# Order of splits, waits and reductions in the attention and the two mixers of a two-block transformer kernel

## The chip, the cores and the metric

The kernel runs on one core of one Trainium2 chip. The metric is the device time of one execution, in microseconds. The core has five engines that run their own instruction lists and meet only at semaphores: PE (TensorE, matrix products), ACT (ScalarE), DVE (VectorE), POOL (GpSimd) and SP (SyncE, which here only starts DMA transfers).

## What is computed

The reference applies two transformer blocks to 256 tokens of width 1024, in float32, batch one. `first_block` has two layers on two streams (256 latent and 256 context tokens): layer 0 is feed-forward, gated MLP, feed-forward; layer 1 is feed-forward, attention, feed-forward. `second_block` has two layers on one stream, each of them feed-forward, mixer, feed-forward. Cut to what the change touches:

```python
def gqa_mix(...):                      # attention of the first block, 8 query heads, 2 key heads, 512 keys
    qkv = h_lat @ w_qkv; kv_c = h_ctx @ w_qkv[:, Q_DIM:]
    q = apply_rope(rms_norm(heads(q)), cos, sin)
    y = softmax(q @ k.T * hd ** -0.5) @ v @ w_o

def mixer(h):                          # one sublayer of the second block
    u = h @ mix_w_in                   # q, k, v, conv a and g, gla q, k, v, gate, rank-16 decay gate
    att  = causal_softmax(rope(rms(q)) @ rope(rms(k)).T) @ v           # 8 heads of 64
    conv = silu(layernorm(causal_conv31(a * sigmoid(g))))              # 256 channels, 31 taps
    gla  = chunked_gated_linear_attention(q, k, v, decays)             # 4 heads, chunks of 64
    return concat(att, conv, gla) @ mix_w_out
```

Each sublayer has a scale, a shift and a gate that come from `silu(c) @ ada_w` (`w_mod` in the first block), nine vectors of 1024 in a layer.

## The kernel before

**Weights.** Every weight matrix is cut into units of 128 by 2048 float32 (1 MB). A unit goes through four steps. SP loads it with two 512 KB transfers into `wraw` (L514). ACT copies it, rounded, into `wh` (the high part, `split_next`, L834). DVE subtracts to get `wl`, the low part (`split_next`, L1219). PE multiplies with three products, high times high, high times low and low times high. There are two slots for each of the three buffers. The load of a unit waits until the low part two units earlier is made (`wlo_done`), the high part waits for the load and for PE to be through with the unit two earlier (`w_used`), and PE waits for the low part (`wlo_done`). `split_next(u)` on ACT or DVE makes the parts of unit u+1; so `unit(i)` of these engines splits one unit ahead of the one that PE's `unit(i)` multiplies.

**Modulation.** The vectors of the next sublayer are summed on DVE in 12 steps for each sublayer: `mod_unit` (L1192) takes 1 MB of `mraw` that SP loaded (L499) and makes two scalar-tensor-tensor instructions. In a mixer the step of index `MIX_MODS` is done in DVE's `unit(idx)`, and SP starts its transfer after the load of two units later. SP's list is in order: each load waits for its slot, and what stands behind it waits as well. `mod_end`, `factors` and `columns` (PE, L2065) turn the sums into columns.

**Order of work.** Nothing is scheduled at run time: each engine's list of a sublayer is written out by hand, in the branch for its kind, between the two feed-forward sublayers.

**Attention** (sublayer 4). Weight units 0 and 1 make keys and values, units 2 to 5 the queries (two heads each), and units 6 to 9 are the output matrix. PE's list (L2546 on) goes `k_t`, `turn_queries(0)`, `unit(4)`, `scores(0)`, `turn_queries(1)`, `unit(5)`, `turn_queries(2)`, `scores(1)`, then the heads. For each pair of query heads DVE's `queries` normalises and rotates (L1748 a sum of squares, then a wait for POOL's `power`, L670, then L1754 to L1764). `maximum` (L1779) takes the row maximum of a head's scores, ACT exponentiates, `normalise` (L1784, L1787) divides. DVE's `unit(4)`, `unit(5)` and `unit(6)` stand between these; `unit(5)` is the split of unit 6 (by the numbers of a unit in the sublayer), `unit(6)` that of unit 7. POOL has only five `power` calls there (L787 to L792).

**Mixer** (sublayers 7 and 10). Twelve input units, then four output units (`out(0)` to `out(3)`, units 12 to 15, L2617 to L2628). PE sums the squares of x (L2646), broadcasts the factors by `rows_of_factors` (L2113, behind POOL's `power`), then `unit(0)`, the small product for the decay gate `cg` (L2655, needs DVE's `cgl`), `unit(1)`, `unit(2)`, and so on, with the products of the three branches between the units. `unit(i)` of PE is L2579 for its first product and L2185 for the others. The convolution's first 128 channels are 31 matrix products with diagonal matrices that ACT makes (L1087). Its second 128 channels are taken by POOL: from `ch_t` on it does, for each of 31 taps, a tensor-scalar (L804) and an addition (L810), with the two `power` calls (L670) for the norms of queries and keys after the taps that `MIX_POOL_TAPS` (L58) gives. When the last addition is done PE transposes the result (L2749). The end of the mixer: DVE normalises the three softmaxes `c`, `b`, `a` (L1895 maximum, L1903, L1904), PE transposes the weights (L2617) and multiplies by v (L2776, L2778), ACT and DVE make the high and low parts of the three results (`hi_...`, L1105; `lo_...`, L1909), and `out(0)` wants `lo_gla`, `out(1)` `lo_conv`, `out(2)` and `out(3)` `lo_att`.

`keep_going(bank, n)` (L2094) makes n products of 128 by 128 whose result nothing reads. `Stages` (L361 for DVE) numbers the marks of an engine: a mark's place in the list is the order in which it is raised.

Of the kernel before, what the change touches and what calls it, by code (L numbers as in the profile page):

```python
# [57 lines left out]
MIX_POOL_TAPS = (11, 16, 31)  # L58
# [121 lines left out]
def program(nc, ins, out, subs):  # L180
    u_end = subs[-1]["n_unit"] + dict(ffn=33, gmlp=36, attn=10, mix=16)[subs[-1]["kind"]]
    with ExitStack() as ctx:
# [89 lines left out]
        def gm_halves(m):  # L272
# [89 lines left out]
                                    "norm_c stats lo_gla pt_c norm_b o_conv max_a pt_b norm_a pt_a lo_conv lo_att")  # L362
# [293 lines left out]
        def _(pool):  # L656
# [72 lines left out]
            for s in subs:  # L729
# [58 lines left out]
                elif s["kind"] == "attn":  # L788
                    load_ln(s)
                    power(nrm1[:, 16:24], 8)  # L790
                    for u in range(4):
                        power(nrm1[:, 4 * u:4 * u + 4], 4)  # L792
                elif s["kind"] == "mix":
# [31 lines left out]
        def _(act):  # L825
# [69 lines left out]
            for s in subs:  # L895
# [77 lines left out]
                elif s["kind"] == "attn":  # L973
# [48 lines left out]
                    unit(3, False)  # L1022
                    square(1)
                    copy_heads(0)
                    unit(4)
# [22 lines left out]
                elif s["kind"] == "mix":  # L1048
# [5 lines left out]
                    def unit(i, to=None):  # L1054

                        split_next(u0 + i)
                        if i == 0:
                            act.wait_ge(mix_full, 160 * (turn + 1) + 32)
                            MA.done("cgh", act.activation(cgh, cg_raw, ACT.Copy))
                        if i < 12:  # L1060
# [9 lines left out]
                            else:  # L1070
                                act.activation(proj[:, :, at:at + CW], src, ACT.Copy).then_inc(pair_free, 1)
                        if i < 10:
# [46 lines left out]
                    unit(3)  # L1119
# [12 lines left out]
                    unit(7)  # L1132
                    MP.wait(act, "heads", turn)
                    stage("q2", act.activation(q2.rearrange("p a b -> p (a b)"), ps[:, 2:4].rearrange("p a b -> p (a b)"), ACT.Copy))
                    unit(8)
# [10 lines left out]
                    high("gla", 6, (6,))  # L1146
                    unit(12)
                    exps("a", 0, p_a[:], 12)
# [17 lines left out]
        def _(dve):  # L1166
# [354 lines left out]
            for s in subs:  # L1521
# [214 lines left out]
                elif s["kind"] == "attn":  # L1736
# [78 lines left out]
                    unit(5)  # L1815
# [3 lines left out]
                    unit(6)  # L1819
                    for h in range(HEADS):  # L1820
# [7 lines left out]
                        if h + 2 < HEADS:  # L1828
                            normalise(h + 2)
                    unit(7)  # L1830
# [7 lines left out]
                elif s["kind"] == "mix":  # L1838
# [5 lines left out]
                    def unit(i):  # L1844
                        if i < 15:
                            split_next(u0 + i)
                        if i == 5:
# [72 lines left out]
                    unit(0)  # L1920
# [3 lines left out]
                    stage("cgl", dve.tensor_tensor(cgl, cg_raw, cgh.bitcast(F32), ALU.subtract))  # L1924
                    if turn == 0:
# [9 lines left out]
                    unit(2)  # L1935
# [5 lines left out]
                    unit(3)  # L1941
                    MA.wait(dve, "softplus", turn)
                    stage("g", dve.tensor_tensor(gg[:], e2[:], e1[:], ALU.subtract))
                    unit(4)
                    sum_squares(0)
                    turn_heads(0)
                    unit(5)
# [3 lines left out]
                    unit(7)  # L1951
# [868 lines left out]
```

## Time and profile before

| what | value |
|---|---|
| median of 3 runs | 3186.78 us (3181.14 to 3188.61) |
| the profiled execution, its own time | 3186.64 us |
| its span, first to last instruction | 3184.9 us |
| PE busy | 3079.7 us, 97% of the span |
| DVE busy | 2031.3 us, 64% |
| ACT busy | 958.2 us, 30% |
| POOL busy | 693.3 us, 22% |
| mean granted TensorE clock | 0.985 |
| attention | about 1664.6 to 1794.2 us of the span |
| first mixer | about 2215 to 2398 us |
| second mixer | about 2800 to 2981 us |

The span is the profiled execution from its first to its last instruction; its own time has 1.7 us more, which lie around the span. [...] The two mixers run from the sum of squares to the last output product, and the attention from its first unit to its last.

### The profile page before, as it was taken

To read this page: it belongs to the slowest core of one execution; us is meant where nothing else is said; L and a number is where in the kernel's file an instruction comes from. 1 tells how busy PE (TensorE), PEld (TensorE's weight loads), DVE (VectorE), ACT (ScalarE), POOL (GpSimd) and SP (SyncE) were. 2 spreads that over 40 slices of the span, in tenths; PEclk is the share of its full clock that TensorE was granted. 3 is DMA by queue.
4 is the path that set the end of the run, shared out by engine and by line. 5 is a ranking of instruction groups with operands and counts; after the bars stand their busy time and mean duration, and the time that the engine had idled before them with its cause. 6 is when DMAs were issued, how large, how long until landed. Compare 5 with 4: busy or idle time off the path is not lost.

```text
span 3184.9 us, 46705 instructions
## 1 busy us (share of the span) xinstructions
PE 3079.7 (97%) x19332; PEld 2738.2 (86%) x19332; DVE 2031.3 (64%) x2134; ACT 958.2 (30%) x1006; POOL 693.3 (22%) x640
## 2 busy tenths in 40 slices
PE   8999999999999999999998999999889999998999
PEld 5888889888888888888887798899879999987899
DVE  5854368766387434774556765775777758668664
ACT  2211122212221122221214333333434343353333
POOL 1311100224022010220100121330742313147110
PEclk9999999999999999999999999999989999999999
DMA  7633235232255332553523496685547869654464
GB/s 258 216 128 93 95 117 197 95 106 80 90 160 173 101 99 87 161 176 119 172 96 131 142 280 205 202 265 172 185 149 233 267 201 272 221 172 172 137 182 158
DMA packets 501667, 522.78 MB, mean 164 GB/s; under 512 B 15732, under 2 KB 433830, under 8 KB 501478
## 3 DMA queue, kind: packets, MB, share of 16 engines
q1 hardware_dynamic: 498536, 513.76, 50.4%
q0 software_dynamic: 2944, 6.32, 0.9%
q8 instruction: 143, 2.34, 0.3%
q14 instruction: 44, 0.36, 0.0%
HBM read 518.97 MB, written 1.05 MB: 163 GB/s over the span
## 4 chain that ended last, share of the span: by engine, by line
PE 85%; DVE 8%; POOL 3%; ACT 2%; issue 1%; DMA 1%; SPq 0%; DVEq 0%; ACTq 0%; POOLq 0%
PE ps L2157 29%; PE ps L2331 15%; PE ps L2243 15%; PE ps L2355 8%; PE ps L2185 6%; PE ps L2222 2%; DVE wl L1219 2%; POOL wst L804 1%; PE ps L2201 1%; POOL lnp L810 1%; PE ps L2269 1%; PE ps L2065 1%; PE ps L2628 1%; ACT wh L834 1%; PE ps L2094 1%
## 5 line engine op out<-in xcount | busy, mean ns | idle before, releaser
L1219 DVE TENSOR_TENSOR wl<-wraw,wh 128x2048 fp32r<-128x2048 f32 x341 | 835.0, 2449 | 586.3 <-ACT wh L834 580.9
L834 ACT ACTIVATE wh<-wraw 128x2048 fp32r<-128x2048 f32 x341 | 652.5, 1914 | 930.5 <-PE ps L2243 387.5
L2157 PE MATMUL ps<-xh,wh 128*128 128x512 f32 (+1 forms) x1504 | 564.5, 375 | 0.7 <-DVE wl L1219 0.4
L2157 PE MATMUL ps<-xl,wh 128*128 128x512 f32 (+1 forms) x1504 | 552.7, 367 | 0.0
L2157 PE MATMUL ps<-xh,wl 128*128 128x512 f32 (+1 forms) x1504 | 551.3, 367 | 0.0
L2331 PE MATMUL ps<-xh,wh 128*128 128x258 f32 x1408 | 403.4, 287 | 5.8 <-DVE xl L1417 4.6
L673 POOL CAST hh<-ht 128x256 f32 (+1 forms) x176 | 140.1, 796 | 1221.3 <-DVE ht L1599 887.0
L2331 PE MATMUL ps<-xh,wl 128*128 128x258 f32 x1408 | 399.5, 284 | 0.0
L2331 PE MATMUL ps<-xl,wh 128*128 128x258 f32 x1408 | 399.3, 284 | 0.0
L1192 DVE SCALAR_TENSOR_TENSOR acc<-mraw,svec,acc 128x1024 f32<-128x1024 f32 x259 | 343.0, 1344 | 15.4 <-DMA mraw<-in_ada_w 10.2
L2157 PEld LDWEIGHTS ps<-xl,wh 128*128 128x128 f32 x1504 | 282.9, 188 | 49.3
L2157 PEld LDWEIGHTS ps<-xh,wl 128*128 128x128 f32 x1504 | 283.3, 188 | 45.1 <-issue 0.7
L2157 PEld LDWEIGHTS ps<-xh,wh 128*128 128x128 f32 x1504 | 283.3, 188 | 44.8 <-issue 1.8
L2331 PEld LDWEIGHTS ps<-xh,wh 128*128 128x128 f32 x1408 | 268.6, 191 | 10.9 <-DVE xl L1417 7.6
L2331 PEld LDWEIGHTS ps<-xl,wh 128*128 128x128 f32 x1408 | 268.9, 191 | 0.0
L2331 PEld LDWEIGHTS ps<-xh,wl 128*128 128x128 f32 x1408 | 268.5, 191 | 0.0
L2185 PE MATMUL ps<-wh,xh 128*128 128x256 f32 x832 | 244.0, 293 | 22.8 <-DVE wl L1219 22.7
L932 ACT ACTIVATE sg<-ps 128x512 f32<-128x512 f32 (+1 forms) x88 | 47.9, 545 | 660.2 <-PE ps L2157 629.2
L2185 PE MATMUL ps<-wh,xl 128*128 128x256 f32 x832 | 238.0, 286 | 0.0
L2185 PE MATMUL ps<-wl,xh 128*128 128x256 f32 x832 | 237.9, 286 | 0.0
L674 POOL TENSOR_TENSOR hl<-ht,hh 128x256 f32 (+1 forms) x176 | 219.2, 1246 | 29.2 <-POOL hh L673 29.2
L2243 PE MATMUL ps<-wh,hh 128*128 128x512 f32 x520 | 205.2, 395 | 1.3 <-DVE wl L1219 1.3
(426 smaller groups left out, 5530.0 us busy)
## 6 DMA issues: line engine op xcount, KB each, us to landing
wraw<-in_ffn_w_in SPq DMA_DIRECT2D x352, 512.0 KB, 5.2
wraw<-in_ffn_w_out SPq DMA_DIRECT2D x176, 512.0 KB, 4.2
mraw<-in_ada_w SPq DMA_DIRECT2D x72, 1024.0 KB, 6.9
mraw<-in_w_mod SPq DMA_DIRECT2D x64, 1024.0 KB, 6.3
wraw<-in_gmlp_w_in SPq DMA_DIRECT2D x48, 512.0 KB, 4.4
wraw<-in_mix_w_in SPq DMA_DIRECT2D x48, 512.0 KB, 4.7
wraw<-in_gmlp_w_out SPq DMA_DIRECT2D x24, 512.0 KB, 3.8
first_w<-in_w_mod SPq DMA_DIRECT2D x8, 1024.0 KB, 11.6
```

The source lines that it names most:

```text
L673: steps.link(pool.tensor_copy(hh[:, where], ht[:, par, 0:width]))
L674: pool.tensor_tensor(hl[:, where], ht[:, par, 0:width], hh[:, where].bitcast(F32), ALU.subtract)\
L834: act.activation(wh[:, slot], wraw[:, slot], ACT.Copy).then_inc(whi_done, 1)
L932: act.activation(sg[:, pair, 0:W], ps[:, 2 * pair, 0:W], ACT.Silu).then_inc(sg_ready, 1)
L1192: op = dve.scalar_tensor_tensor(out=to, in0=mraw[:, q % 2, jj], scalar=svec[:, v, 2 * q + jj:2 * q + jj + 1], in1=biasrow[:] if q == jj == ...
L1219: dve.tensor_tensor(wl[:, slot], wraw[:, slot], wh[:, slot].bitcast(F32), ALU.subtract)\
L2157: m = pe.matmul(ps[:, bank, 0:width], a, b, start=k == p == 0, stop=k == KD - 1 and p == 2)
L2185: m = pe.matmul(to, a, b, start=k == p == 0, stop=k == KD - 1 and p == 2)
L2222: m = pe.matmul(ps[:, 2 * t + half], a, b, start=False, stop=i == kk == 1 and p == 2, skip_group_check=i == 0)
L2243: m = pe.matmul(ps[:, bank0 + 2 * t + half], a, b, start=start and kk == p == 0, stop=stop and kk == 1 and p == 2, skip_group_check=not st ...
L2331: m = pe.matmul(ps[:, 2 * pair + r, 0:XW], a, b, start=n == p == 0, stop=n == KD - 1 and p == 2)
L2355: m = pe.matmul(ps[:, j, 0:T], a, b, start=i == kk == p == 0, stop=i == KF // 2 - 1 and kk == 1 and p == 2, skip_group_check=i == 5)
```

## The change

It touches the attention's and the mixers' branches on all five engines' lists except SP's, which is left as it is written. There are six edits.

1. Attention: PE does `unit(4)` and `unit(5)` earlier, ACT makes the high part of unit 5 before it squares the keys, and the low parts of units 6 and 7 are made by POOL, after its last `power`, no longer by DVE, which waits for both before its `unit(7)`.
2. Mixer, start: `keep_going(3, 8)` before and `keep_going(3, 14)` after `rows_of_factors`; `cgh` (ACT) and `cgl` (DVE) are made ahead of the first split.
3. Mixer, splits: units 3 and 4, 6, and 8 and 9 are split ahead of modulation, turning of heads and other work on DVE, and 4 and 9 ahead on ACT. `qk` is marked one step earlier (on `kt`).
4. POOL's two `power` calls come after 9 and 14 taps in place of 11 and 16. The second half's 31 taps stay on POOL, as they were.
5. Mixer, end: DVE takes `maximum("a")` behind `normalise("c")`, ACT makes the exponentials of `a` ahead of its `unit(12)`, DVE normalises `a` right behind `o_conv`.
6. Mixer, end: DVE's split of unit 13 (its `unit(12)`) moves behind the two `turned_weights`, its modulation behind `low("conv")`.

```diff
-MIX_POOL_TAPS = (11, 16, 31)
+MIX_POOL_TAPS = (9, 14, 31)
...
@@ POOL, attention
                         power(nrm1[:, 4 * u:4 * u + 4], 4)
+                    for i in (6, 7):
+                        u = s["n_unit"] + i
+                        pool.wait_ge(whi_done, u + 1)
+                        pool.tensor_tensor(wl[:, u % 2], wraw[:, u % 2], wh[:, u % 2].bitcast(F32), ALU.subtract)\
+                            .then_inc(wlo_done, 1)
@@ ACT, attention
                     unit(3, False)
+                    split_next(u0 + 4)
                     square(1)
                     copy_heads(0)
-                    unit(4)
+                    unit(4, False)
@@ ACT, mixer
-                        split_next(u0 + i)
                         if i == 0:
                             act.wait_ge(mix_full, 160 * (turn + 1) + 32)
                             MA.done("cgh", act.activation(cgh, cg_raw, ACT.Copy))
+                        if split:
+                            split_next(u0 + i)
...
+                        if i == 2:
+                            split_next(u0 + 3)
...
-                    unit(3)
+                    unit(3, False)
...
                     unit(7)
+                    split_next(u0 + 8)
                     MP.wait(act, "heads", turn)
...
-                    unit(8)
+                    unit(8, False)
...
+                    exps("a", 0, p_a[:], 12)
                     unit(12)
-                    exps("a", 0, p_a[:], 12)
@@ DVE, attention
                     normalise(0)
-                    unit(5)
                     maximum(1)
                     queries(3)
                     normalise(1)
-                    unit(6)
...
+                    dve.wait_ge(wlo_done, u0 + 9)
                     unit(7)
@@ DVE, mixer
-                    unit(0)
...
                     stage("cgl", dve.tensor_tensor(cgl, cg_raw, cgh.bitcast(F32), ALU.subtract))
+                    unit(0)
...
-                    unit(2)
+                    split_next(u0 + 2)
+                    split_next(u0 + 3)
                     MP.wait(dve, "z", turn)
...
-                    unit(3)
+                    modulation(2)
                     MA.wait(dve, "softplus", turn)
                     stage("g", dve.tensor_tensor(gg[:], e2[:], e1[:], ALU.subtract))
+                    modulation(3)
                     unit(4)
                     sum_squares(0)
+                    split_next(u0 + 5)
                     turn_heads(0)
-                    unit(5)
+                    modulation(5)
                     sum_squares(1)
                     unit(6)
                     turn_heads(1)
-                    unit(7)
+                    split_next(u0 + 7)
+                    split_next(u0 + 8)
+                    modulation(7)
...
-                    dve.tensor_tensor(kt[:], c_k, e2[:], ALU.mult)
+                    stage("qk", dve.tensor_tensor(kt[:], c_k, e2[:], ALU.mult))
+                    modulation(8)
...
-                    unit(8)
                     MP.wait(dve, "qk_t", turn)
...
                     normalise("c", p_c, 0)
+                    maximum("a", 0, 4, 12)
                     MP.wait(dve, "conv", turn)
...
                     normalise("b", p_b, 8)
-                    unit(12)
...
                     stage("o_conv", last)
-                    maximum("a", 0, 4, 12)
+                    normalise("a", p_a[:], 12)
                     turned_weights("b", 2, slice(2, 4))
-                    normalise("a", p_a[:], 12)
                     turned_weights("a", 0, slice(0, 2))
+                    split_next(u0 + 12)
                     low("conv", 4, (2,))
+                    modulation(12)
                     unit(13)
@@ PE, attention
+                    unit(4)
                     turn_queries(0)
-                    unit(4)
+                    unit(5)
                     scores(0)
                     turn_queries(1)
-                    unit(5)
                     turn_queries(2)
                     scores(1)
@@ PE, mixer
                     m.then_inc(ss_ready, 1)
+                    keep_going(3, 8)
                     rows_of_factors(s)
+                    keep_going(3, 14)
                     unit(0)
```

## Rows read from the trace of the kernel before

**Rows 1.** The page's chain that ended last: share of the span by engine.

```profile
PE 85%; DVE 8%; POOL 3%; ACT 2%; issue 1%; DMA 1%; SPq 0%; DVEq 0%; ACTq 0%; POOLq 0%
```

**Rows 2.** The chain of waits in attention: start us, us, what.

```profile
1713.21 2.29 DVE wl L1219
1727.98 2.20 DVE wl L1219
1732.25 1.02 POOL nrm L670
1737.48 2.20 DVE wl L1219
1739.68 1.15 DVE negm L1779
```

**Rows 3.** POOL's instructions of the kind that splits: ns min/median/max, and their shapes.

```profile
L674 POOL TENSOR_TENSOR hl<-ht,hh x176: 725/1285/3362, 66.6 to 3122.4; 128x256 f32 x110, 128x512 f32 x66
...
L787 POOL TENSOR_TENSOR gm_h<-ht,gm_h x8: 1293/2268/3423, 748.3 to 789.5; 128x512 fp32r<-128x512 f32 x8
```

**Rows 4.** POOL's and DVE's timeline at 282 us: start us, us.

```profile
282.22 1.29 POOL L674 TENSOR_TENSOR hl<-ht,hh 128x512 f32 x1 [0.16 <-POOL hh L673]
...
282.29 3.37 DVE L1219 TENSOR_TENSOR wl<-wraw,wh 128x2048 fp32r<-128x2048 f32 x1 [1.02 <-ACT wh L834]
```

**Rows 5.** The timeline of DVE and POOL at 789 us.

```profile
789.45 2.29 DVE L1219 TENSOR_TENSOR wl<-wraw,wh 128x2048 fp32r<-128x2048 f32 x1
...
789.47 3.42 POOL L787 TENSOR_TENSOR gm_h<-ht,gm_h 128x512 fp32r<-128x512 f32 x1
```

**Rows 6.** What PE waited for in the first mixer: us in total, times, longest.

```profile
PE ps L2185 <- DVE wl L1219: 11.2, 3, 4.3
PE ps L2617 <- DVE p_a L1904: 5.9, 1, 5.9
...
PE ps L2655 <- DVE cgl L1924: 1.1, 1, 1.1
```

**Rows 7.** What PE waited for in the second mixer.

```profile
PE ps L2185 <- DVE wl L1219: 9.8, 3, 4.1
...
PE ps L2655 <- DVE cgl L1924: 1.6, 1, 1.6
```

**Rows 8.** What DVE waited for in the first mixer.

```profile
DVE proj L1881 <- POOL nrm L670: 6.4, 2, 4.9
```

**Rows 9.** PE's timeline and its granted clock (seventh figure of a window).

```profile
1670.18 3.73 PE L2094 MATMUL ps<-ident,ones 128*128 128x128 f32 x32
...
2218.00:2223.00 5.00, 2.36 (x10) 1.98 (x9) 1.52 (x5) 0.91 (x2) 1.65 (x2) 0.50 0.09 6
```

**Rows 10.** POOL's timeline in the first mixer: first tap, last tap.

```profile
2249.59 1.22 POOL L804 TENSOR_SCALAR lnp<-lnp 128x256 f32<-128x256 f32 x1 [19.41 <-ACT lnp L1082]
...
2344.17 0.73 POOL L810 TENSOR_TENSOR lnp<-lnp,wst 128x256 f32<-128x256 f32 x1
```

**Rows 11.** POOL's last tap in the second mixer.

```profile
2926.62 0.72 POOL L810 TENSOR_TENSOR lnp<-lnp,wst 128x256 f32<-128x256 f32 x1
```

**Rows 12.** PE's transposes of the convolution, first and second mixer.

```profile
2350.37 0.60 PE L2749 MATMUL ps<-ident,lnp 128*128 128x128 f32 x4
...
2931.21 0.60 PE L2749 MATMUL ps<-ident,lnp 128*128 128x128 f32 x4
```

**Rows 13.** DVE's timeline at the end of the first mixer.

```profile
2366.49 2.29 DVE L1219 TENSOR_TENSOR wl<-wraw,wh 128x2048 fp32r<-128x2048 f32 x1
...
2386.03 2.60 DVE L1192 SCALAR_TENSOR_TENSOR acc<-mraw,svec,acc 128x1024 f32<-128x1024 f32 x2
2388.55 1.22 DVE L1909 TENSOR_TENSOR xl<-ps,xh 128x1024 fp32r<-128x1024 f32 x1
```

**Rows 14.** SP's transfers there, and the page's time to landing (last figure).

```profile
2369.65 0.43 SPq L499 DMA_DIRECT2D mraw<-in_ada_w  x1
...
mraw<-in_ada_w SPq DMA_DIRECT2D x72, 1024.0 KB, 6.9
```

More of the change, by code:

```diff
@@ L361, in program @@
         MV = Stages(sem("mix_dve"), "cgl cg_t h absz g sum_q q_turned sum_k k_turned qk k2 kt_t states max_c o_copy max_b oc "
-                                    "norm_c stats lo_gla pt_c norm_b o_conv max_a pt_b norm_a pt_a lo_conv lo_att")
+                                    "norm_c max_a stats lo_gla pt_c norm_b o_conv norm_a pt_b pt_a lo_conv lo_att")
         MP = Stages(sem("mix_pe"), "cg z h_t sums heads qk_t scores o s_c s_b conv s_a omt pt_c pt_b pt_a convt pv")
@@ L1053, in stage, with unit @@
                         MA.wait(act, name, turn)
-                    def unit(i, to=None):
-                        split_next(u0 + i)
+                    def unit(i, split=True):
                         if i == 0:
@@ L1846, in unit, with modulation @@
                             split_next(u0 + i)
+                        modulation(i)
+                    def modulation(i):
                         if i == 5:
@@ L1960, in _ @@
                                                       in1=e3[:], op0=ALU.mult, op1=ALU.mult)
-                    stage("qk", op)
+                    steps.link(op)
                     MP.wait(dve, "heads", turn)
                     stage("k2", dve.tensor_copy(k2.rearrange("p a b -> p (a b)"), ps[:, 4:6].rearrange("p a b -> p (a b)")))
-                    unit(8)
                     MP.wait(dve, "qk_t", turn)
```

## Prediction, made before the changed kernel was run

> **What bounds the kernel now.** I read the page's chain first: 85% of the span is PE's own work, 8% DVE's, 3% POOL's [rows 1]. So the kernel is bound by PE, save for the two kinds of stage that the change touches. Then I read the chain of waits inside the attention, where two low parts (2.20 us each) and a row maximum of DVE stand on it [rows 2]: there DVE sets the pace. Then what PE waited for in each mixer. It lost 11.2 us in three waits for a low part in the first mixer, 9.8 us in the second, and 1.1 and 1.6 us for `cgl` [rows 3, 4]. That is what edits 2 and 3 aim at. Last I asked what is late next: POOL's taps run without a gap from 2249.59 to 2344.90 in the first mixer [rows 5], and PE's transposes of their result start at 2350.37 there and at 2931.21 in the second [rows 6], where the taps end at 2927.34 [rows 7]. PE can be earlier there by 5.5 and 3.9 us and no more, however many waits are removed ahead of it.
>
> **Attention (edit 1).** PE's `unit(5)` moves ahead of `scores(0)` and `unit(4)` ahead of `turn_queries(0)`. DVE's low part of unit 5 starts now at 1713.21, because ACT makes its high part only after other work; with the high part made early it follows the turning of the queries at about 1709.5. The first maximum comes behind PE's scores, which stand behind one unit more, so I keep only 1.1 of these 3.7 us. DVE then drops two low parts. The first, at 1727.98, gives 0.6 us, not 2.2, since `maximum(1)` needs `scores(1)`, which PE does only behind `turn_queries(2)`; the second, at 1737.48, gives its 2.2 us. So the third maximum, which ends at 1740.83 [rows 2], would end 3.8 us earlier (1.07 + 0.58 + 2.20), at 1737.0, if POOL's part cost nothing.
>
> It costs something. POOL has a 128x256 subtraction in 0.725 us at least, a 128x512 one in 1.285 [rows 8], so 256 columns more are 0.56 us, and 2048 columns (eight times 256) are 0.725 + 7 x 0.56 = 4.65 us, an estimate; four times the 128x512 one is 5.1, the upper bound. POOL starts on them when its last `power` is done, about 1731.5 (now 1732.25 + 1.02, 1.65 earlier), just where DVE turns the last queries, with two-input instructions on SBUF. The trace shows what such a pair does: at 282.22 POOL began a subtraction of 1.29 us, DVE's low part began 0.07 us later and took 3.37 us in place of 2.29, so 1.08 longer [rows 9]. The other way about, a POOL subtraction that began behind a DVE low part took 3.42 us where 1.28 to 1.29 is the least [rows 8, 10]. So the one that comes second stands until the first is through. The longest such block of DVE in any row is one POOL instruction, about 1.3 us; if nothing longer than this happens, the two subtractions cost DVE 2.6 us and the edit still gives 3.8 - 2.6 = 1.2 us. If the block lasts as long as POOL's instruction, DVE loses 4.65 twice, 9.3 us less the little that lies beside DVE's own waits: the queries' last turning ends at about 1744, `normalise(1)` at 1745, the third maximum at 1746.2 in place of 1740.83, 5.4 us later. Between these ends I take the longer one, because the rows show the block to follow the length of POOL's instruction and to let DVE in only at its end. The head loop behind it is paced by the same DVE chain, so the delay stays: **+5.4 us**, bounds -3.8 and +6.4 (5.1 us for each subtraction).
>
> The Trainium skill, "SBUF — State Buffer", section "Who interferes with whom", has the same as a rule: the port pair that DVE and GpSimd share is an exclusive lock, held for the whole instruction, and a DVE instruction with two SBUF inputs contends with a GpSimd one that reads SBUF. By that rule the block is the full length, as in the sum above; the trace agrees at 1.3 us (3.37 against 2.29), and no row of it shows 4.65. The rule speaks against this edit; by the other reading of the rows (1.3 us each) the edit would come to -1.2.
>
> **Mixers, start (edit 2).** 22 products are added in each mixer. 32 of their instructions took 3.73 us at full clock [rows 11], 0.117 each, and a product is two of them, so 22 cost 5.1 us at the most, if they stand in PE's way. They don't quite: PE waits there for POOL's `power` and DVE's first columns. The clock granted in the first mixer is at its lower level, 1.2 GHz (0.50), from 2218 to 2223 already [rows 11], before the place where the products go. I put the later end of `unit(0)` at +1.4 us if the clock stays down and -0.3 if they bring it back. `cgl` ahead of the split removes 1.1 and 1.6 us of waiting [rows 3, 4]. Together nothing, between +3 and -2 in each mixer.
>
> **Mixers, splits (edits 3 and 4).** The split of the next unit stood behind modulation (2.6 us) or turned heads; with it ahead, the 11.2 and 9.8 us of waiting mostly go, some 9 us. POOL's taps don't shorten: 31 taps in 95.3 us are 3.1 us each [rows 5], and they start with `ch_t`, on ACT, which now has one split (1.9 us) ahead of it. The first `power` two taps earlier takes what DVE waits for in turning heads (6.4 us [rows 12]) away or leaves it to the split that stands there now; it moves nothing on POOL. So the end of taps comes 1.6 us later in the first mixer and 0.5 in the second, and PE's transposes can be earlier by 5.5 - 1.6 = 3.9 and 3.9 - 0.5 = 3.4 us. Of this the cold start of a unit behind a wait may take 1.5 in the first.
>
> **Mixers, end (edits 5 and 6).** The maximum and exponentials of `a` moved ahead remove PE's wait of 5.9 us for `p_a` [rows 3], and PE reaches `out(1)` some 5 us earlier. But the low part of unit 13, which starts at 2366.49 now, comes behind both `turned_weights`: by my count of DVE's instructions at 2376.5, ten us later, and ends at 2378.8. It gates SP: the load of unit 15 and then `mraw` of the last modulation go out right behind it, `mraw` now at 2369.65, 0.9 us after the low part's end, to land 6.9 us later by the page's median [rows 13, 14]. So it goes out at 2379.7 and lands at 2386.6; the modulation takes 2.60 us, to 2389.2, and the low part of the attention's result, queued behind it on DVE, 1.22 us, to 2390.4. Now it ends at 2388.55 + 1.22 = 2389.8 [rows 13], and `out(2)` starts at 2390.5 when PE is through with `out(1)`. So `out(2)` starts when it did: what PE gains in `out(0)` and `out(1)` it gives back in one wait of some 5 us, and behind such a wait it may run at half clock at first, which I put at 1.5 us: a unit takes 5.9 us at full clock and 7.4 where part of it is at half. In the second mixer `out(2)` starts 1.1 us later than this now, and I keep that as gain.
>
> **The sum.** What is gained ahead of the transposes (3.9 and 3.4 us) is kept at the end, since everything behind them shifts with them. In the first mixer I take off 1.5 us for the cold unit ahead of them and 1.5 for a cold `out(2)`: 3.9 - 3.0 = 0.9 us. In the second I take off 1.5 for `out(2)` and add the 1.1 of its tail: 3.4 - 1.5 + 1.1 = 3.0 us. Together -3.9 us, bounds -9.4 (5.5 + 3.9, all the room there is) and +3 (edit 2's upper price in one mixer, nothing gained in the other). With +5.4 from attention: +1.5. The profiled execution took 3186.64 us with a span of 3184.9; it stands 0.14 under the median of 3186.78, so both give **3188** (3186.6 + 1.5). A measurement of this kernel can tell about 0.2% from no change, 6.4 us, so this is no change.
>
> **Rivals.** (A) Faster: POOL's subtractions cost DVE little (they fall into DVE's waits, or it gets in between), and the mixers give all of POOL's room. For it: the longest block in the rows is 1.3 us, and DVE waits in that stretch for `power`. Against it: the rows' blocks are as long as POOL's instruction. It gives 3186.6 - 1.2 - 9.4 = 3176, or 3173.4 with -3.8 in place of -1.2. With the mixers at -3.9 it is 3182, still no change. 0.25. (B) Slower: POOL's taps become the mixer's end. DVE's work is packed denser, each low part that meets a tap holds it up (one more meeting is 1.8 us by the tap's mean of 3.1), the taps end later and PE waits for `cacc`. It decides from the point where the taps take more than about 99 us (95.3 + the 3.9 that are left). Then a mixer gives +1.5 to +2 and the whole is 3186.6 + 5.4 + 3.5 = 3195.5. For it: the room is 5% of the taps' time. Against it: what is moved is the same work at other times. 0.18. (C) The change doesn't do what it says at the start: the products are put where the clock is already down, cost 1.5 us each mixer, and bring nothing. That alone gives 3191; it stays inside no change and is part of the forecast's range.
>
> **Chances.** Forecast (give and take) 0.57, A 0.25, B 0.18. From the same cases: faster by over 0.2% (below 3180.4) 0.25, within 0.57, slower (above 3193.2) 0.18. Range: up to 3196 for B, down to 3176 for A's first price; the deepest part of A is left out. The forecast's own range is 3181 to 3193.
>
> **What would show it.** In the attention: two POOL subtractions of 4.6 to 4.7 us with DVE instructions of 4 to 5 us beside them where 0.4 stands now, and the third maximum 5 us later. If DVE's stay below 1.5 us, that step is wrong and the stage is shorter. In the mixers: PE's waits for `wl` down from 11.2 and 9.8 to under 3; the transposes 2 to 4 us earlier against the mixer's start, with POOL's last tap within 1 us of them; a new PE wait of some 5 us before `out(2)` for `lo_att`, with DVE behind `mraw`. If the transposes come 6 us earlier, POOL's taps got shorter and the forecast is too high. A wait of PE or ACT for `cacc` is B.

## The result, and the profile after

In the prediction some groups of rows are named by numbers other than those they stand under. There, [rows 3] is group 6, 4 is 7, 5 is 10, 6 is 12, 7 is 11, 8 is 3, 9 is 4, 10 is 5, 11 is 9 and 12 is 8; 1, 2, 13 and 14 are the same. From here on every number is that of the group as it stands.

The changed kernel took **3196.13 us** (median of 7 runs, 3188.18 to 3202.43), the kernel before 3183.57 (7 runs, 3180.05 to 3189.15). The ratio is **1.0035**, 95% interval 1.0024 to 1.0047, so 11 us slower (7.6 to 15). The forecast was 3188 and no change. 3196.13 lies at the upper end of the full range, which stood at 3196 for the slower rival, and outside the forecast's own range of 3181 to 3193. The change is clear of the 0.2% that the text asked for: it came out as the slower case, which had 0.18. The profiled execution took 3194.63 us with a span of 3192.9, 8.0 us more than that of before; the parts below add up to these 8.0. Single executions of one kernel differ by some microseconds, as the ranges show.

The page of the changed kernel, busy time and the chain that ended last:

```profile
PE 3090.6 (97%) x19420; PEld 2749.6 (86%) x19420; DVE 2037.4 (64%) x2132; ACT 958.3 (30%) x1006; POOL 707.2 (22%) x642
...
PE 84%; DVE 7%; POOL 4%; ACT 2%; DMA 1%; issue 1%; SPq 0%; DVEq 0%; ACTq 0%; POOLq 0%
```

POOL's share of the chain rose from 3% [rows 1] to 4%. To see where the time went I took the starts of ACT's high parts, which come in the same order and number in both kernels, and subtracted. In the profiled executions, between the same two high parts around attention: 192.13 us before, 198.79 after (**+6.7**). From the first sum of squares of a mixer to a high part in the feed-forward behind it: 192.61 and 192.60 in the first (**0.0**), 194.01 and 195.70 in the second (**+1.7**); in the second mixer the stretch ends one high part later than in the first, so only kernels are to be compared in it, not the two mixers. The rest (-0.4) lies in stages whose code is the same.

**Attention.** The chain of waits of the kernel before, at the turning of the last queries:

```profile
1733.29 0.70 DVE ql L1754
...
1734.01 0.42 DVE tm L1759
```

and of the changed kernel, from the second maximum on:

```profile
1728.17 1.22 DVE negm L1789
...
1730.33 1.02 POOL nrm L670
1731.37 5.00 DVE ql L1764
1736.39 4.60 DVE tm L1769
1740.99 0.34 DVE tm L1770
```

and POOL's timeline in the same stretch:

```profile
1731.30 9.41 POOL L796 TENSOR_TENSOR wl<-wraw,wh 128x2048 fp32r<-128x2048 f32 x2
```

Two DVE instructions that took 0.70 and 0.42 us in the kernel before take 5.00 and 4.60, side by side with POOL's two subtractions, which are 4.7 us each. The attention was 1.7 us early when it began (1632.07 against 1633.77 at the high part ahead of it), so the third maximum, which ends at 1745.17 and ended at 1740.83 [rows 2], is 6.0 us late against its own start.

**Mixers.** What PE waited for, first mixer:

```profile
PE ps L2646 <- DVE xl L1921: 10.5, 2, 6.2
PE ps L2203 <- DVE wl L1229: 5.1, 3, 4.0
```

and second mixer:

```profile
PE ps L2646 <- DVE xl L1921: 9.2, 2, 4.9
PE ps L2203 <- DVE wl L1229: 5.0, 3, 4.0
PE ps L2769 <- POOL lnp L815: 1.9, 1, 1.9
```

The waits for a low part of a weight fell from 11.2 and 9.8 us [rows 6, 7] to 5.1 and 5.0, and those for `p_a` and `cgl` are gone. The prediction's sign was a fall to under 3 us. One wait of 4.0 us stays in each mixer: DVE makes the low part of unit 7 behind `turn_heads(0)`, which still waits for POOL's `power` (4.65 us in the first mixer; both waits for `power` there come to 8.3 us, and were 6.4 before [rows 8]), and PE waits for that low part. In their place stand waits for `xl` in the output units (10.5 and 9.2 us, one of 2.9 before) and one for POOL's taps. POOL's last tap and PE's transposes of it, first mixer, and then the second:

```profile
2349.02 0.72 POOL L815 TENSOR_TENSOR lnp<-lnp,wst 128x256 f32<-128x256 f32 x1
...
2351.73 0.60 PE L2769 MATMUL ps<-ident,lnp 128*128 128x128 f32 x4
...
2936.94 0.72 POOL L815 TENSOR_TENSOR lnp<-lnp,wst 128x256 f32<-128x256 f32 x1
...
2937.81 0.63 PE L2769 MATMUL ps<-ident,lnp 128*128 128x128 f32 x4 [1.95 <-POOL lnp L815]
```

Against the mixer's first sum of squares (at 2214.79 and 2221.10; 2800.14 and 2806.44) the transposes moved from 135.58 to 130.63 us in the first mixer (4.95 earlier) and from 131.07 to 131.37 in the second (0.3 later). Then the end of the first mixer, on DVE, SP and PE:

```profile
2378.75 2.28 DVE L1229 TENSOR_TENSOR wl<-wraw,wh 128x2048 fp32r<-128x2048 f32 x1
...
2381.90 0.43 SPq L499 DMA_DIRECT2D mraw<-in_ada_w  x1
...
2390.01 2.60 DVE L1202 SCALAR_TENSOR_TENSOR acc<-mraw,svec,acc 128x1024 f32<-128x1024 f32 x2 [3.29 <-DMA mraw<-in_ada_w]
2392.53 1.22 DVE L1921 TENSOR_TENSOR xl<-ps,xh 128x1024 fp32r<-128x1024 f32 x1
...
2393.90 0.55 PE L2646 MATMUL ps<-xh,wh 128*128 128x256 f32 x1 [6.22 <-DVE xl L1921]
```

Read from the top: the late low part of unit 13, the transfer behind it, DVE's wait for the transfer, the low part of the attention's result behind that, and PE's wait for it. From silu's end (ACT's silu of the gate, behind the last input unit; at 2358.66, and 2357.30 before) to the same high part in the feed-forward behind the mixer it is 55.04 us where it was 50.10: the 4.95 us gained at the transposes are given back to the last tenth. In the second mixer it is 52.63 against 51.24.

### The profile page after: what moved, and what is told of

Read it like the earlier page. It is cut to its first block, busy times and chain, and to the rows that moved or that the text cites. A ratio compares the mean times of both kernels' runs of the same rounds, so it can differ in the third digit from the quotient of the medians.

```text
span 3192.9 us, 46882 instructions
## 1 busy us (share of the span) xinstructions
PE 3090.6 (97%) x19420; PEld 2749.6 (86%) x19420; DVE 2037.4 (64%) x2132; ACT 958.3 (30%) x1006; POOL 707.2 (22%) x642
## 3 DMA queue, kind: packets, MB, share of 16 engines
HBM read 518.97 MB, written 1.05 MB: 163 GB/s over the span
## 4 chain that ended last, share of the span: by engine, by line
PE 84%; DVE 7%; POOL 4%; ACT 2%; DMA 1%; issue 1%; SPq 0%; DVEq 0%; ACTq 0%; POOLq 0%
PE ps L2175 29%; PE ps L2349 15%; PE ps L2261 15%; PE ps L2373 8%; PE ps L2203 6%; PE ps L2240 2%; POOL wst L809 2%; DVE wl L1229 2%; POOL lnp L815 2%; PE ps L2219 1%; PE ps L2646 1%; PE ps L2112 1%; PE ps L2287 1%; PE ps L2083 1%; ACT wh L839 1%
```

## The experiments

Twelve kernels ran. "Attention" is the stretch above; "mixers" are the two stretches from the first sum of squares; "end" is from silu's end to a high part behind (in the second mixer one earlier than that of "mixers"). All three come from one profiled execution of each. The ratios are of timed runs against the kernel before on the same chip.

| kernel | ratio (95% interval) | attention | mixers | end, 1st and 2nd |
|---|---|---|---|---|
| before | 1 | 192.1 | 192.6, 194.0 | 50.1, 51.2 |
| changed | 1.0035 (1.0024 to 1.0047) | 198.8 | 192.6, 195.7 | 55.0, 52.6 |
| e1 edit 1 alone | 1.0024 (1.0011 to 1.0036) | 197.4 | 191.6, 190.3 | 51.0, 50.1 |
| e2 low parts on DVE | 1.0022 (1.0012 to 1.0033) | 192.0 | 193.6, 197.5 | 55.0, 51.5 |
| e3 unit 13 early | 0.9988 (0.9979 to 0.9997) | 197.6 | 184.7, 189.4 | 47.1, 46.6 |
| e4 no keep_going | 1.0034 (1.0021 to 1.0048) | 197.6 | 187.9, 198.5 | 51.9, 53.8 |
| e5 = e2 + e3 | 0.9974 (0.9964 to 0.9985) | 191.9 | 185.5, 188.1 | 46.1, 47.1 |
| e6 POOL after q_3 | 1.0041 (1.0029 to 1.0053) | 198.7 | 191.6, 199.2 | 54.9, 53.2 |
| e7 = e5, old attention | 0.9978 (0.9969 to 0.9987) | 192.1 | 185.6, 189.2 | 46.1, 46.1 |
| e8 = e5, ch_t first | 0.9968 (0.9955 to 0.9980) | 190.8 | 185.8, 189.3 | 46.8, 46.1 |
| e9 edits 2 to 4 alone | 1.0007 (0.9996 to 1.0018) | 192.5 | 188.5, 195.8 | 51.1, 51.1 |
| e10 edit 5 alone | 0.9986 (0.9976 to 0.9996) | 193.7 | 187.6, 191.6 | 48.3, 48.3 |
| e11 = e5, 25 taps | 0.9952 (0.9936 to 0.9967) | 192.0 | 178.2, 188.9 | 47.2, 47.2 |
| e12 eight pieces | 1.0026 (1.0014 to 1.0037) | 195.3 | 192.4, 195.6 | 54.7, 52.7 |

How far one execution of a mixer can be trusted: before and e1 have the same mixers and differ by 1.0 and 3.7 us; the changed kernel, e2, e6 and e12 have the same ones and span 2.0 us in the first (191.6 to 193.6) and 3.6 in the second (195.6 to 199.2). Attention is steadier (191.9 to 192.5 wherever it should be as before, but for 190.8 in e8 and 193.7 in e10, where its code gives no reason). With the whole of edit 1 it spans 197.4 to 198.8 in four kernels (changed, e1, e3, e4), 197.9 in the mean, against 192.6 in the four with none of it (before, e7, e9, e10). So the cost of edit 1 in attention is 5.3 us by these means, and the +6.7 of the single pair is at its upper end. The mixers of the changed kernel, e2, e6 and e12 come to 389.5 us together in the mean, those of before and e1 to 384.3: +5.3, where the single pair shows +1.7.

### Attention: is it POOL's block, and how long is it?

**e1.** The kernel before with edit 1 and nothing else.

> The kernel before with edit 1 alone (attention: unit 5 moved forward, two low parts on POOL). Theory (a full-length block of DVE by POOL's two subtractions): the stage is 6 to 7 us longer than before, DVE instructions of 4.5 to 5 us in it, and the whole 6 to 7 us slower, ratio 1.0020. Rival (what the profile of the changed kernel shows in attention is drift of one execution, and the loss is in the mixers): the whole stays within 2 us of before, ratio 1.000 to 1.0006.

1.0024, 7.6 us, with attention at 197.4: the theory. Edit 1 by itself is some two thirds of the whole loss.

**e2.** The changed kernel, with POOL's loop removed:

```diff
-                    for i in (6, 7):
-                        u = s["n_unit"] + i
-                        pool.wait_ge(whi_done, u + 1)
-                        pool.tensor_tensor(wl[:, u % 2], ...).then_inc(wlo_done, 1)
...
                     normalise(0)
+                    unit(5)
                     maximum(1)
                     queries(3)
                     normalise(1)
+                    unit(6)
...
-                    dve.wait_ge(wlo_done, u0 + 9)
```

> The changed kernel with the low parts of units 6 and 7 back on DVE; PE's and ACT's new order stays. Theory (the block is the loss): the attention's third maximum comes 6 to 7 us earlier than in the changed kernel, and the whole is about 3189 us against its 3196. Rival (the new order, with unit 5 ahead of the first scores, is the loss): less than 2 us comes back, about 3195.

Attention fell from 198.8 to 192.0. All of its loss is POOL's part, and the new order of unit 5 is worth nothing by itself. Beside this, e2 shows what the rest of the change does alone: with attention as before it is still 1.0022, so edits 2 to 6 cost 7 us (3.8 to 10.5). The whole came to 3191.6, 2.6 us above what I expected (its second mixer ran 1.8 us longer than the changed kernel's in this execution).

**e7** asks the same from the other side: e5 (below) without any of edit 1.

> As e5, and also PE's and ACT's order in attention as before (edit 1 gone altogether). Theory (unit 5 forward gives nothing by itself, since the first maximum is earlier by 1.1 us and the second isn't): within 1 us of e5 in attention and in all, about 3177. Rival (unit 5 forward gives 1 to 3 us that POOL's block hid): 2 us or more slower than e5.

192.1 against 191.9, medians 3177.15 and 3177.73. The rival falls.

**e6.** POOL works when DVE has turned its last queries.

```diff
+                    AV.wait(pool, "q_3", 0)
                     for i in (6, 7):
```

> The changed kernel, but POOL's two subtractions wait until DVE has turned the last queries (mark q_3). Theory (DVE is blocked only where it reads two inputs from SBUF or moves SBUF to SBUF at twice the rate): the two long waits on DVE's chain move from the turning to the head loop; normalise (SBUF to SBUF) may stand for 4 us, the maxima and low parts that read PSUM don't; of the 6.6 us in attention some 3 come back, total about 3193. Rival 1 (any DVE instruction is blocked, so it doesn't matter where POOL works): attention stays within 1 us of 198.8. Rival 2 (nothing in the head loop is blocked): attention at 190 to 192, total 3189.

The theory's size was wrong: nothing came back (198.7; 1.0041). POOL's and DVE's timeline:

```profile
1738.62 9.13 POOL L797 TENSOR_TENSOR wl<-wraw,wh 128x2048 fp32r<-128x2048 f32 x2 [3.19 <-DVE ql L1775]
...
1738.78 9.26 DVE L1798 TENSOR_SCALAR ht<-ht,den 128x512 f32<-128x512 f32 x2
```

The block doesn't need two inputs. `normalise` has one input, from SBUF to SBUF, two instructions that take 0.88 us together elsewhere, and they took 9.26: one for each of POOL's. Since the very next instruction of DVE in the head loop is of that kind, moving POOL's work behind the turning only changes who stands. The rival that any instruction is blocked has the right length, but this run doesn't prove it: no maximum or low part that reads PSUM fell beside POOL's work here. In e12 they do, and they are not blocked (below).

**e12.** The same work of POOL in pieces.

```diff
-                        pool.tensor_tensor(wl[:, u % 2], wraw[:, u % 2], wh[:, u % 2].bitcast(F32), ALU.subtract)\
-                            .then_inc(wlo_done, 1)
+                        for c in range(8):
+                            cut = slice(c * 256, (c + 1) * 256)
+                            op = pool.tensor_tensor(wl[:, u % 2, cut], wraw[:, u % 2, cut], wh[:, u % 2, cut].bitcast(F32), ALU.subtract)
+                        op.then_inc(wlo_done, 1)
```

> The changed kernel, with each of POOL's two subtractions in attention cut into eight of 128x256. Theory (the port is held for one instruction and handed over at its end): DVE's blocked instructions are 0.5 to 0.8 us longer each, not 4.6; the six of the turning and the two of normalise stand once each, so DVE loses 5 to 6 us, not 9, and attention is 194 to 196 us against 198.8. Rival 1 (the block costs what POOL works in all, however it is cut): 198 to 200. Rival 2 (POOL is always the one that waits when its pieces are short): 191 to 192.

195.3: inside the theory's 194 to 196. DVE and POOL take turns, as the chain of waits shows (0.83 and 0.88 us for what takes 0.34 and 0.42), and POOL needs 13.07 us for its sixteen pieces where the two whole ones took 9.41:

```profile
1735.61 1.22 DVE ql L1766
1736.83 0.02 issue
1736.85 0.83 DVE tm L1771
1737.68 0.88 DVE tm L1772
```

```profile
1735.54 13.07 POOL L798 TENSOR_TENSOR wl<-wraw,wh 128x256 fp32r<-128x256 f32 x16
```

So the block lasts as long as the one POOL instruction, and the length of that instruction is the price. 3.5 us of the 6.7 come back, or some 2.5 against the mean of 197.9; DVE doing the work itself gives all of it (e2).

This run also settles what e6 left open. DVE's maximum and a low part, both of which read PSUM, fall beside POOL's pieces:

```profile
1743.66 1.21 DVE L1791 TENSOR_REDUCE negm<-ps 128x2 f32<-128x1024 f32 x1
...
1746.66 0.42 DVE L1836 TENSOR_TENSOR xl<-ps,xh 128x256 fp32r<-128x256 f32 x1 [1.79 <-ACT xh L1051]
```

```profile
1744.28 2.77 POOL L798 TENSOR_TENSOR wl<-wraw,wh 128x256 fp32r<-128x256 f32 x4
```

They take 1.21 and 0.42 us, the same as where POOL is idle (1.22 and 0.42), and POOL's four pieces take 0.72 each. So not any instruction of DVE is blocked: those with two inputs in SBUF are, and `normalise`, and these two are not. The four pieces also give the price of the cutting: they follow each other at 0.69 us, which makes 11.0 for sixteen, an estimate, of the 13.07.

### The end of the mixers: what holds out(2)?

**e3.** One line moved back.

```diff
                     normalise("b", p_b, 8)
+                    split_next(u0 + 12)
...
                     turned_weights("a", 0, slice(0, 2))
-                    split_next(u0 + 12)
                     low("conv", 4, (2,))
```

> The changed kernel with DVE's low part of unit 13 back behind normalise b; the rest of the mixer's end as changed. Theory (the late low part holds SP's load and mraw, and mraw the last modulation and lo_att): mraw goes out some 8 us earlier, PE's wait of 4.9 to 6.2 us before out(2) goes, out(2) runs in 5.9 us and not 8.6, and each mixer is 6 us shorter: about 3184 in all. Rival (DVE's own work at the end is the limit): the low part only moves 2.3 us of DVE's time forward, lo_att comes no earlier, and the whole stays within 2 us of 3196.

0.9988 against 1.0035: 15 us for one line, where I had expected 12. The end of the first mixer now:

```profile
2373.72 2.28 DVE L1229 TENSOR_TENSOR wl<-wraw,wh 128x2048 fp32r<-128x2048 f32 x1
...
2376.88 0.43 SPq L499 DMA_DIRECT2D mraw<-in_ada_w  x1
...
2389.30 2.60 DVE L1202 SCALAR_TENSOR_TENSOR acc<-mraw,svec,acc 128x1024 f32<-128x1024 f32 x2
...
2393.18 0.36 PE L2646 MATMUL ps<-xh,wh 128*128 128x256 f32 x1 [1.05 <-DVE xl L1921]
```

Against silu's end (2363.12 here, 2358.66 in the changed kernel) the transfer goes out at 13.8 us and not 23.2, the last modulation has no wait, and `out(2)` starts at 30.1 and not 35.2. It also runs at the clock's upper level. The granted clock of the stretch of `out(2)`, first the changed kernel and then e3, is the seventh figure:

```profile
2393.90:2402.50 8.60, 8.60 (x51) 8.60 (x51) 2.05 (x1) 0.00 (x0) 0.00 (x0) 0.65 0.44 122
```

```profile
2393.20:2399.10 5.90, 5.90 (x51) 5.90 (x51) 2.29 (x1) 0.94 (x1) 0.00 (x0) 1.00 0.43 112
```

The ends are shorter by 7.9 and 6.0 us (55.0 to 47.1 and 52.6 to 46.6); in the first mixer 5.2 of them are the earlier start of `out(2)` and 2.7 its faster run.

**e5.** e2 and e3 together.

> The changed kernel with both: low parts 6 and 7 on DVE, and the low part of unit 13 back behind normalise b. Theory (two separate losses that add): attention as in the kernel before (192 us between the same high parts), mixers as with the early split alone, about 3177 us, ratio 0.9975. Rival (the mixers' length hangs on something else, such as the moment at which they start): they fall back to 180 us each, and the whole is about 3190.

3177.7, ratio 0.9974: the two losses are separate and add, and the version beats both kernels.

**e10.** Edit 5 alone, with unit 13 where the kernel before has it.

> The kernel before with edit 5 alone (maximum and exponentials of a moved ahead), the low part of unit 13 where it was. Theory (edit 5 is the part that pays): silu's end to the end of the mixer is 44 to 45 us, as with the early split, against 47.7 before: 3 us less in each, 3178 in all. Rival (PE's wait of 5.9 us for p_a goes in full): 6 us in each, 3172.

0.9986, 4.5 us, and ends of 48.3 and 48.3 against 50.1 and 51.2. That is 1.8 and 2.9 us less, where I had 3 in each; the 44 to 45 and the 47.7 that I wrote are counted to an earlier point (the first product of the feed-forward). e5 and e7 have 46.1 to 47.1. What their ends have on top is that the modulation of unit 13 comes behind `low("conv")`, the other half of edit 6, which would be worth 1 to 2 us in each mixer; but these kernels also have edits 2 to 4, and no run takes that half alone, so this is argued and not shown.

### The front of the mixers: what do the splits give?

**e9.** Edits 2 to 4, with attention and the end as before.

> The kernel before with edits 2 to 4 alone (start and splits of the mixers, powers two taps earlier); attention and the mixer's end as before. Theory (POOL's taps bound what these edits can give): the transposes of the convolution start 128.5 to 132 us behind the first sum of squares, within 0.2 to 2 us of POOL's last tap, 5 us earlier than before in the first mixer and 0 to 1 in the second; 4 us off in all, 3180. Rival (removing 9 us of PE's waits in each mixer shows in full once the end is left alone): 12 us or more off, 3171.

A miss in size: 1.0007, 0.9996 to 1.0018, so between 1.3 us faster and 5.7 slower, where I had 4 us faster. The rival of 12 us is out. The transposes do what the theory says. First and second mixer:

```profile
2340.33 0.73 POOL L810 TENSOR_TENSOR lnp<-lnp,wst 128x256 f32<-128x256 f32 x1
...
2341.20 0.63 PE L2763 MATMUL ps<-ident,lnp 128*128 128x128 f32 x4 [0.19 <-POOL lnp L810]
...
2923.50 0.63 PE L2763 MATMUL ps<-ident,lnp 128*128 128x128 f32 x4 [1.92 <-POOL lnp L810]
```

At 130.38 us behind the sum of squares in the first mixer, against 135.58, and PE has come to wait for POOL in both.

**e11.** e5 with POOL's last six taps left out of the computation.

```diff
-MIX_POOL_TAPS = (9, 14, 31)
+MIX_POOL_TAPS = (9, 14, 25)
...
-                                if tap == CONV_K:
+                                if tap == MIX_POOL_TAPS[-1]:
```

> As e5, but POOL takes 25 of the second half's 31 taps; the last six are left out of the computation. Theory (POOL's taps are the mixer's bound at the transposes): POOL ends 11 to 18 us earlier, the transposes start at about 124 us behind the first sum of squares, where PE gets there by itself, 5 to 6 us earlier than in e5, with no wait for the taps; 10 to 12 us off in all, 3166. Rival (PE or DVE is the bound there, and POOL only near it): within 2 us of e5, 3176.

0.9952: 7 us less than e5, not 10 to 12. In the first mixer POOL ends at 2338.40, and PE's transposes start at 2347.92, 124.0 us behind the sum of squares, within 0.2 us of where PE was ready in e5 (130.66 less its wait of 6.49). In the second they start at 2924.87, 130.0 us behind, with POOL through since 2909.01: no gain at all. The difference is the clock in the stretch ahead of them, first mixer, then second:

```profile
2328.00:2348.00 20.00, 19.64 (x156) 16.92 (x156) 17.20 (x23) 3.31 (x9) 9.67 (x9) 1.00 0.45 158
2899.00:2925.00 26.00, 24.42 (x159) 21.08 (x160) 18.32 (x25) 3.62 (x9) 9.39 (x8) 0.80 0.36 123
```

PE gets there at 124 us where the last 20 us ahead run at the clock's upper level (2.4 GHz), and at 130 where the last 26 us run at the lower (1.2 GHz) for a part; 1.2 us of the six are a longer wait of PE at the head of that stretch, 1.58 for 0.36, for which the profile shows no cause. POOL ends at 128.6 to 132.5 in the twenty profiled mixers with edits 2 to 4 and 31 taps, and in seventeen of them the transposes start within 0.25 us of its last tap; in the other three within 2.0. So the two bounds lie close together, POOL's mostly last, and how long PE waits for it says only how fast PE came: 6.5 us in the first mixer of e5, 1.7 in the second.

**e8.** e5 with `ch_t` made ahead of the high part of unit 4.

```diff
                         if i == 2:
+                            turned_channels()
                             split_next(u0 + 3)
...
```

> As e5, and ACT makes ch_t ahead of the high part of unit 4 and not behind it, so that POOL's taps start 1.9 us earlier. Theory (the taps' end bounds each mixer's transposes in the second mixer, where PE waited 1.9 us for cacc, and not in the first, where 2.0 us were left): 0 to 2 us from the second mixer, none from the first, about 3176. Rival (the taps are the end in both): 2 us from each, about 3173.

Inconclusive: 0.9968 against 0.9974, with intervals that overlap. The experiment did not do what it was meant to: the first tap came at 36.4 and 33.6 us behind the sum of squares (33.3 and 33.7 in e5), because in e5 ACT's high part runs while PE is still turning the channels, and costs POOL nearly nothing; here ACT waits 1.55 us for PE in its place. My 1.9 us were never there to be won. It is the fastest median of all that compute everything (3173.47), but not shown to be faster than e5.

**e4.** The changed kernel without the added products.

> The changed kernel without both keep_going calls. Theory (the products are put where the clock is already down and stand in front of the factors): each mixer's start is 0 to 2 us earlier, unit(0) slower (7.5 to 8 us, not 5.9), and the whole within 2 us of 3196. Rival (they save the clock for the units behind them): 3 us or more slower, 3199 to 3201.

3195.94 against 3196.13: nothing in the whole, either way. In the changed kernel `unit(0)` runs in 5.91 us (7.98 and 7.53 before, 7.80 and 7.51 in e4) and starts later for the products in front of it. It ends 16.4 and 18.0 us behind the sum of squares, and at 16.4 twice in e4: in the first mixer the two cancel, in the second the products cost 1.7 us. In the kernels with the products it ends at 14.8, 16.4 or 18.0. The profile of e4 has one mixer 4.7 us shorter and one 2.8 us longer than the changed kernel's, so it says no more.

## Why the prediction was right or wrong, point by point

**Attention, right in mechanism and nearly in size.** I put +5.4 us; it is +6.7 in the profile (6.0 by the third maximum), 5.3 by the means of four kernels each, and 7.6 (3.5 to 11.5) by e1. The two terms: POOL's instruction, an estimate of 4.65 us from 0.725 and 1.285 [rows 3], is 4.7, and the block has that full length (5.00 for 0.70, 4.60 for 0.42), of which no row of before showed more than 1.1 [rows 4]. The reading "about 1.3 us each" is refuted by the trace after, and e12 shows that the length follows POOL's instruction. At the third maximum the block cost 8.5 us (4.30 + 4.18), where I had 9.2. What was too high was the other term. I gave the new order and the two low parts taken from DVE 3.8 us; they gave 2.4 (8.5 - 6.0). The first maximum came 1.15 us earlier, as said. The step that failed is the gain of 1.07 + 0.58 at `maximum(1)`: it ended only 0.2 earlier in all, at 1729.39 against an old 1729.61 (1731.32 less the 1.7 by which the stage began early). DVE waited 3.05 us for `scores(1)`. PE, with `unit(5)` already behind it, had stood 6.0 us until DVE had turned the queries, and then ran in part at the clock's lower level (mean granted clock 0.60): its `turn_queries(2)` took 1.12 us in place of 0.66, and `scores(1)` 2.97 where the first scores took 1.88. In the kernel before, PE came to the same place without a wait. The rule that the Trainium skill gives ("SBUF — State Buffer", "Who interferes with whom"), an exclusive lock for the whole instruction, agrees with 5.00, 4.60 and 9.26 us; that a tensor-scalar with one tensor input, from SBUF to SBUF, can be caught as well is in the same section, and e6 shows it.

**Front of the mixers, half right.** I said that POOL's taps allow the transposes 3.9 and 3.4 us and no more, and took 1.5 off in the first for a cold unit. Measured: 4.95 and -0.3. Of the signs, "2 to 4 us earlier" and "POOL's last tap within 1 us" of the transposes failed in the first mixer (the gap is 1.99), and the first of them in the second. The first mixer's cold unit did not cost what I took off. In the second the step that failed is "POOL's taps don't shorten": nor did they stay. There the phase took 95.5 us in place of 93.1, and it began 1.6 us later (35.7 behind the sum of squares, 34.1 before), where I had 0.5. With the added products `unit(0)` ended at 18.0 and not at 16.4 as in e4, where the phase began at 33.7: so edit 2, which I had put at nothing, delays the taps here. The phase ended at 131.22, just past the 131.07 at which PE had started the transposes, and PE waited 1.95 us for it. In the first mixer it began 0.5 us earlier, where I had 1.6 later, and took 94.4 in place of 95.3. The longer phase is rival B's: POOL's 30 additions (L815, L810 before) take 33.9 us in sum where they took 30.6, each at least 0.72. That DVE's two-input work, packed denser, is what holds them up is argued from the blocks above, not shown by a run. I had put the point from which it decides at 99 us, from the longer phase of the first mixer; in the second it is 93.1 + 3.9 less the later start of 1.6, so 95.4, and was just reached. e9 and e11 confirm the bound and add what I had missed, PE's own arrival, at 124 to 130 us by the clock, close ahead of it. In time, e9 puts edits 2 to 4 at +2.2 us (-1.3 to +5.7), where the sum has -5.8.

**End of the mixers, right in mechanism and too small.** The chain came as written: the low part of unit 13, foreseen ten us later, was 10.9 later against silu's end (20.1 against 9.2); then `mraw`, a wait of DVE for it (3.29), `lo_att`, a wait of PE. I foresaw "some 5 us" of wait and got 6.22 and 4.88. Two terms were mis-sized. `out(2)` was to start where it did, 33.2 us behind silu; it started at 35.2, since the modulation could begin only at 31.3 and not 29.3 (the transfer went out 0.8 us later than foreseen, and took 8.1 us rather than 6.9). And the cold unit cost 2.7 us (8.6 against 5.9), not 1.5. So the end lost 4.9 us in the first mixer, where I had 1.5, and 1.4 in the second, where I had 0.4.

**The sum.** Predicted: +5.4 - 0.9 - 3.0 = +1.5. In the profile: +6.7 + 0.0 + 1.7 = +8.4, less 0.4 elsewhere. The signs of the losses and their places were right. The step that failed is the sum of the mixers, -3.9 us: it is +1.7 in the single pair of profiles, +5.3 by the means, and +7 (3.8 to 10.5) by e2's timed runs. It counted nearly the whole of POOL's room as gain and priced the wait it had itself found at the end at 1.5 us. e3 shows that this one line was worth more than all else in the change. The slower rival, attention's +5.4 and the mixers' +3.5, gave 3195.5 us, which is near what was measured; but its mechanism decided only in the second mixer (+0.3 us at the transposes), and the late transfer did the rest; that the number fits is in part luck. The median of the timed runs is a further 3 us above the profile's difference. That is of the size by which single executions differ, and e2 and the means point at the mixers for it.

## What to carry to other kernels

A helper engine whose instructions block those of the engine it relieves takes the relieved time back for as long as its own, slower, instruction lasts: before moving a 2.3 us instruction that then takes 4.7, look for what stands on the chain beside it, and if it must be moved, cut it small. When a split is moved behind other work, follow what its completion releases on the transfer queue, and what is queued behind that transfer's user; here one instruction moved by eleven microseconds cost fifteen in two stages. And before counting a removed wait as gain, ask what arrives last at the next meeting point, and how far off it is: in the second mixer PE's waits for low parts and `cgl` fell by 6 us, and the transposes came no earlier.

## What was not expected of the hardware

A tensor-scalar from SBUF to SBUF with one tensor input was blocked as long as a tensor-tensor: two of them took 9.26 us beside two POOL subtractions of 4.6 us. Sixteen POOL pieces took 13.07 us in turns with DVE where two whole ones took 9.41, some 1.6 us of it for the cutting and the rest for the turns, but the chain on DVE gains 2.5 to 3.5 us. A maximum and a low part that read PSUM took their usual 1.21 and 0.42 us beside POOL's pieces. A unit of 48 products took 8.6 us right behind a wait of 6.22 and 5.9 behind one of 1.05, with a mean granted clock of 0.65 and 1.00.
